# Second and third norm of a decoder step on one Trainium2 core: squares made block by block beside the products, two ones-products in place of eight, query product with the contraction outermost

## What is computed

```python
h += W_o [ attention heads | pooling groups ]( W_in rms_norm(h, norm_mix) )
h += mem_attend(rms_norm(h, norm_mem), mk, mv, w_mq, w_mo)     # second norm; q = xn @ w_mq, 4 heads of 128
tok = rms_norm(h, norm_ffn)                                    # third norm
h += moe(tok, router_w, router_b, w_up, b_up, w_down, b_down)  # top 4 of 32 experts, width 1024
y = rms_norm(h, norm_final)

def rms_norm(x, g):
    return x * rsqrt(mean(x * x, axis=-1) + EPS) * g
```

## Time and profile before

| | us |
|---|---|
| median of 3 runs | 1297.07 (1296.37 to 1297.4) |
| profiled execution, its own time | 1295.67 |
| its span in the trace | 1293.4 |
| PE busy | 1192.0 (92% of the span) |
| DVE busy | 389.3 (30%) |
| ACT busy | 223.8 (17%) |
| mean granted TensorE clock | 0.966 of full speed |

### The profile page before, as it was taken

How to read it: one execution, slowest core, us unless ns; L and a number is a source line. 1 busy time by engine, 2 the same in 40 slices (tenths; PEclk the granted TensorE clock), 3 DMA queues, 4 the chain that set the end, 5 groups by cost and what they waited for, 6 DMA issues and landing times.

```text
span 1293.4 us, 15539 instructions
## 1 busy us (share of the span) xinstructions
PE 1192.0 (92%) x6102; PEld 539.4 (42%) x6103; DVE 389.3 (30%) x921; ACT 223.8 (17%) x430; POOL 52.4 (4%) x67
## 2 busy tenths in 40 slices
PE   7997789798599999999899999999899999999997
PEld 5774555576433333333233333333333332333342
DVE  2376960241521222223122222312222231312222
ACT  1245640132111010111101011110101111110112
POOL 2117000000000000000000000000000000000000
PEclk9998698999689999999999999999999999999999
DMA  9234356306959999999999999999999999999993
GB/s 375 78 125 170 132 194 230 139 1 258 403 231 409 426 427 427 428 426 428 428 424 427 428 428 429 427 426 429 426 426 428 427 427 427 428 427 428 428 427 130
DMA packets 44220, 452.15 MB, mean 350 GB/s; under 512 B 5484, under 2 KB 6408, under 8 KB 18023
## 3 DMA queue, kind: packets, MB, share of 16 engines
q1 hardware_dynamic: 41711, 437.19, 80.8%
q0 software_dynamic: 2432, 13.89, 2.8%
HBM read 448.68 MB, written 2.61 MB: 349 GB/s over the span
## 4 chain that ended last, share of the span: by engine, by line
PE 70%; DVE 14%; DMA 10%; ACT 3%; issue 3%; POOL 0%; SPq 0%; DVEq 0%; ACTq 0%
PE psum L1194 26%; PE psum L1231 16%; DMA mem<-in_w_up_dram 10%; PE psum L1181 4%; PE psum L691 4%; DVE mem L2077 2%; PE psum L1148 2%; PE psum L989 2%; PE psum L896 2%; DVE mem L2069 2%; DVE mem L2072 1%; PE psum L1172 1%; DVE mem L1865 1%; ACT mem L1611 1%; DVE mem L2074 1%
## 5 line engine op out<-in xcount | busy, mean ns | idle before, releaser
L1194 PE MATMUL psum<-mem 128*64 128x512 f32 x2048 | 460.6, 601 | 12.8 <-DMA mem<-in_w_up_dram 6.3
L1194 PEld LDWEIGHTS psum<-mem 128*64 128x64 f32 x2048 | 144.7, 138 | 304.3 <-issue 291.0
L1231 PE MATMUL psum<-mem 128*64 128x512 f32 x1024 | 236.9, 600 | 0.0
L1231 PEld LDWEIGHTS psum<-mem 128*64 128x64 f32 x1024 | 66.6, 136 | 133.2 <-issue 112.6
L2069 DVE TENSOR_SCALAR mem<-psum 128x512 f32<-128x512 f32 x32 | 22.1, 692 | 272.6 <-PE psum L1194 272.6
L1611 ACT ACTIVATE mem<-mem 128x512 f32<-128x512 f32 x32 | 20.1, 629 | 470.7 <-DVE mem L2069 470.7
L1350 ACT ACTIVATE mem<-psum 128x512 f32<-128x512 f32 (+5 forms) x137 | 67.7, 545 | 153.6 <-PE psum L691 44.7
L2064 DVE TENSOR_TENSOR mem<-mem,psum 128x528 f32<-128x528 f32 x64 | 45.1, 704 | 143.7 <-PE psum L1181 143.7
L1181 PE MATMUL psum<-mem 128*128 128x264 f32 x256 | 65.5, 398 | 0.0
L1140 PE MATMUL psum<-mem 128*64 128x512 f32 x256 | 62.2, 607 | 2.4 <-DVE mem L2047 2.4
L2054 DVE TENSOR_SCALAR mem<-mem 128x64 f32<-128x64 f32 x102 | 25.6, 310 | 128.7 <-PE psum L1166 99.4
(11 more groups left out here) (310 smaller groups left out, 931.6 us busy)
## 6 DMA issues: line engine op xcount, KB each, us to landing
mem<-in_w_up_dram SPq DMA_DIRECT2D x128, 2048.0 KB, 30.5
mem<-in_w_down_dram SPq DMA_DIRECT2D x64, 2048.0 KB, 30.7
mem<-in_w_in_dram SPq DMA_DIRECT2D x8, 868.0 KB, 14.6
mem<-in_w_o_dram SPq DMA_DIRECT2D x1, 4096.0 KB, 14.4
mem<-in_cache_mem_k_dram SPq DMA_DIRECT2D x1, 4096.0 KB, 16.7
mem<-in_cache_mem_v_dram SPq DMA_DIRECT2D x1, 4096.0 KB, 14.2
mem<-in_w_mk_dram SPq DMA_DIRECT2D x1, 2048.0 KB, 8.7
mem<-in_w_mv_dram SPq DMA_DIRECT2D x1, 2048.0 KB, 14.8
```

Of the source, the lines that this page charges most:

```text
L1194: ins = pe.matmul(ps[64 * o:64 * o + 64, :], lhs, w[:, k % 2, g * 1024 + o * 512:g * 1024 + (o + 1) * 512], start=False, stop=(k == 7), sk ...
L1231: ins = pe.matmul(pso[64 * o:64 * o + 64, :], lhs, w[:, k % 4, o * 512:(o + 1) * 512], start=(k == 0), stop=(k == 7), skip_group_check=True)
```

## The change

ACT squares one feature block as soon as its sum is in `hT`, in eight instructions, and runs a small Sqrt ahead of them. DVE adds the squares of blocks 1 to 6 onto block 0, between its additions of the products. PE makes two ones-products, over the sum of blocks 0 to 6 and over block 7. Every scaling of the second and third norm now raises `xn_ready`; the query product has the feature block as its outer loop and waits block by block, the router product likewise in its first row tile.

```diff
--- before.py
+++ after.py
@@ -680,10 +680,10 @@
             def sum_squares(n):
 
                 b = take(pe, "ss", n)
-                pe.wait_ge(S("squares"), n - 1)
-                for k in range(KD):
-                    ins = pe.matmul(b[:, 0:NT], ones, xnT[:, k, :], start=(k == 0), stop=(k == KD - 1))
-                done(ins, "ss", n)
+                pe.wait_ge(S("squares_added"), (n - 1) * (KD - 2))
+                pe.matmul(b[:, 0:NT], ones, xnT[:, 0, :], start=True, stop=False)
+                pe.wait_ge(S("squares"), (n - 1) * KD)
+                done(pe.matmul(b[:, 0:NT], ones, xnT[:, KD - 1, :], start=False, stop=True), "ss", n)
 
             def z_rows(b, m, k):
 
@@ -1000,14 +1000,15 @@
                                            mknat[:, t, h * P:(h + 1) * P], ident)
                 done(ins, "mkT", g)
             sum_squares(2)
-            pe.wait_ge(S("xn_ready"), KD + 1)
             pe.wait_ge(S("w_mq_in"), 16)
-            for h in range(MH):
-                b = take(pe, "mq", h)
-                for k in range(KD):
-                    ins = pe.matmul(b[:, 0:NT], w_mq_sb[:, k, h * P:(h + 1) * P], xnT[:, k, :],
+            mqb = [take(pe, "mq", h) for h in range(MH)]
+            for k in range(KD):
+                pe.wait_ge(S("xn_ready"), KD + k + 1)
+                for h in range(MH):
+                    ins = pe.matmul(mqb[h][:, 0:NT], w_mq_sb[:, k, h * P:(h + 1) * P], xnT[:, k, :],
                                     start=(k == 0), stop=(k == KD - 1))
-                done(ins, "mq", h)
+                    if k == KD - 1:
+                        done(ins, "mq", h)
             for g in range(2):
                 wait_drained(pe, "mkT", g)
             for h in range(MH):
@@ -1090,10 +1091,11 @@
                 done(ins, "mo", m)
             sum_squares(3)
             b = take(pe, "rl")
-            pe.wait_ge(S("xn_ready"), KD + 2)
             pe.wait_ge(S("router_in"), 32)
             for r in range(3):
                 for k in range(KD):
+                    if r == 0:
+                        pe.wait_ge(S("xn_ready"), 2 * KD + k + 1)
                     ins = pe.matmul(b[0:ROWS[r], r * NE:(r + 1) * NE], xnT[:, k, r * P:r * P + ROWS[r]], rw_sb[:, k, :],
                                     start=(k == 0), stop=(k == KD - 1))
             done(ins, "rl")
@@ -1352,10 +1354,11 @@
                     ins.then_inc(drained(*job), 1)
                 return ins
 
-            def squares(n, waits):
-                for w in waits:
-                    wait_drained(act, *w)
-                act.activation(xnT, hT, ACT.Square).then_inc(S("squares"), 1)
+            def squares(n, tag):
+                act.activation(stat[:, 60:61], stat[:, 61:62], ACT.Sqrt)
+                for m in range(KD):
+                    wait_drained(act, tag, m)
+                    act.activation(xnT[:, m, :], hT[:, m, :], ACT.Square).then_inc(S("squares"), 1)
 
             def root(n):
                 b = result(act, "ss", n)
@@ -1529,7 +1532,7 @@
             for t in range(2):
                 b = result(act, "mv", t)
                 copy(mv[:, t, :], b[:, :], "mv", t)
-            squares(2, [("wo", m) for m in range(KD)])
+            squares(2, "wo")
             act.wait_ge(S("stored_mk"), 32)
             wait_filled(act, "mkT", 1)
             root(2)
@@ -1567,7 +1570,7 @@
             for s in range(2):
                 b = result(act, "smv", s)
                 copy(os_[:, s, :], b[:, :], "smv", s)
-            squares(3, [("mo", m) for m in range(KD)])
+            squares(3, "mo")
             root(3)
             for r in range(3):
                 w = ROWS[r]
@@ -1653,16 +1656,27 @@
                 for k in range(KD):
                     ins = dve.scalar_tensor_tensor(out=xnT[:, k, :], in0=hT[:, k, :], scalar=gains[:, gain + k:gain + k + 1],
                                                    in1=factor, op0=ALU.mult, op1=ALU.mult)
-                    if gain == 0:
-                        ins.then_inc(S("xn_ready"), 1)
-                return ins
+                    ins.then_inc(S("xn_ready"), 1)
 
             def norm(n, gain):
 
                 wait_drained(dve, "ss", n)
                 dve.reciprocal(temp[:, 2, :], temp[:, 3, :]).then_inc(S("rstd_ready"), 1)
                 dve.wait_ge(S("rstd_ready"), n - 1)
-                scale_tokens(gain, temp[:, 2, :]).then_inc(S("xn_ready"), 1)
+                scale_tokens(gain, temp[:, 2, :])
+
+            def add_product(n, tag, m):
+
+                b = result(dve, tag, m)
+                dve.tensor_tensor(hT[:, m, :], hT[:, m, :], b[:, 0:NT], ALU.add).then_inc(drained(tag, m), 1)
+                if 1 < m:
+                    add_squares(n, m - 1)
+
+            def add_squares(n, m):
+
+                dve.wait_ge(S("squares"), (n - 2) * KD + m + 1)
+                dve.tensor_tensor(xnT[:, 0, :], xnT[:, 0, :], xnT[:, m, :], ALU.add).then_inc(S("squares_added"), 1)
+                dve.wait_ge(S("squares_added"), (n - 2) * (KD - 2) + m)
 
             def ties(x, thr, k, gt, eq, cum, cnt, need, parts=P):
 
@@ -1913,8 +1927,7 @@
             dve.tensor_copy(mixT[0:64, 0:4, TP:NT], v[:, :, :, 0])
             dve.tensor_copy(mixT[64:128, 0:4, TP:NT], v[:, :, :, 1]).then_inc(drained("spo"), 1)
             for m in range(KD):
-                b = result(dve, "wo", m)
-                dve.tensor_tensor(hT[:, m, :], hT[:, m, :], b[:, 0:NT], ALU.add).then_inc(drained("wo", m), 1)
+                add_product(2, "wo", m)
             dve.wait_ge(S("stored_un"), 32)
             for m in range(KD):
                 wait_drained(dve, "wo", m)
@@ -1964,8 +1977,7 @@
                     ins = dve.tensor_copy(omT[:, h, TP + 4 * s:TP + 4 * s + 4], v[:, :, h])
                 ins.then_inc(drained("omt", s), 1)
             for m in range(KD):
-                b = result(dve, "mo", m)
-                dve.tensor_tensor(hT[:, m, :], hT[:, m, :], b[:, 0:NT], ALU.add).then_inc(drained("mo", m), 1)
+                add_product(3, "mo", m)
             for m in range(KD):
                 wait_drained(dve, "mo", m)
             norm(3, 16)
```

## The result

The changed kernel takes 1281.4 us (median of 4 runs, 1279.69 to 1282.87), the kernel before beside it 1296.72 us (4 runs, 1295.36 to 1297.4). The ratio is 0.9881, 95% interval 0.9868 to 0.9894: 1.2% faster, some 15 us. The forecast was 1281.1 us, from 1278.0 to 1285.5. The profiled execution is the slowest of the four, 1282.87 us with a span of 1281.0, so its trace accounts for 12.4 us of span, and not for 15; no trace shows the rest.

A forecast was written before the change was run, and what follows sets the result against it. Expert weight loading bounds the kernel, so the chain ahead of the first refill counts in full. Second norm 9.6 plus third norm 6.7 less bias wait 0.3 gives 16.0 us: 1297.07 to 1281.1 us, range 1278 to 1285.5.

The forecast's parts named there:

- The bound: Expert stage: weight loading holds it, so the end moves only with PE finishing its first part of weights.
- Second norm: Relay up to the query product: squares, ones-products, table load and scalings leave the chain, 8.5 us without the clock's term.
- The clock: PE around the second norm's gap: shorter idling may keep the clock up, gain 1.1 us, bounds 0 and 2.2.
- Third norm: Relay up to the router product: 7.25 us less, 6.7 us after 0.5 us given back in that product.
- the pace of the scalings: Router product's first row tile: runs only as fast as scalings arrive, giving back 0.5 us.
- Bias rows: Start of the expert stage: PE reaches `b_up` 6.7 us earlier with 6.4 us of slack, so waits 0.3 us.
- Rival (a): Start of the expert stage: late `b_up` or `b_down` swallows the third norm's gain, 1287.5 us; 7%.
- From the bias rows to the refill: First expert products: clock counted only as chance, about 1.8 us either way.
- (b): Both norms: additions of squares on DVE hold the ones-products, 2 us in each norm, 1285 us; 3%.
- (c): Expert loop: something other than the stream's start sets its end and takes all gain back, 1297 us; 1%.
- the constant: From PE's first finished part of weights to the end: time stays the same, no size given.
- The fourth: Second norm to attention: clock falls and stays down, query product 28.5 us in place of 16.4, whole 1320 us; 3%.

The follow-up runs named there:

- second_only: Changed kernel with the third norm kept as before, so only the second norm is changed; 1285.84 us, ratio 0.9924 to the kernel before.
- third_only: Changed kernel with the second norm kept as before, so only the third norm is changed; 1290.87 us, ratio 0.9953 to the kernel before.
- heads_outer: Changed kernel with the query product's head outermost again and one wait for all eight scalings; 1287.98 us, ratio 0.9930 to the kernel before.
- late_table: Changed kernel without the small Sqrt ahead of the squares, so the table loads behind the last square; 1282.14 us, ratio 0.9894 to before.
- bias_first: Changed kernel with `b_up` issued ahead of the first eight weight parts, no filler; 1280.83 us, ratio 0.9886 to the kernel before.
- eight_ones: Changed kernel with eight ones-products, each waiting for its own square, and no additions of squares; 1282.75 us, ratio 0.9899 to before.
- warm_both: Changed kernel with six useless ones-products as filler ahead of both query and router product; 1280.85 us, ratio 0.9886 to the kernel before.

## Why the prediction was right

**The bound.** Right, and the best supported step: the table above.

**Second norm.** The forecast was 8.5 us to the start of the query product; measured 8.36 (13.88 to 5.52 us). The square of a block took 0.42 us (0.39 taken). The additions of squares took 0.42 to 0.43 and held PE for 0.15. The table load was worth 1.29 and the seven scalings 2.78. The ones-products went from 3.80 to 1.13 us, 2.67 less where 2.85 was forecast. But that size holds only against the kernel before: with the squares made block by block, eight products would have cost only 2.28 us more in the second norm and 1.41 in the third, so a part of the term, half of it in the third norm, belongs to the squares.

**The clock.** I took 1.1 us of gain, the middle of 0 and 2.2; the 2.2 is the product's 16.40 us less 4 x 3.56 = 14.24 us. In the trace before, the clock fell to 0.50 at 253.5, 4.3 us after PE's last work and 2.9 ahead of the product. No run shows a gain of 1.1: in the trace after it was a loss of 0.8 us, outside my bounds. I had priced a fallen clock as "no worse than before", but here it fell at 247.0, just ahead of the query product, and covered 5.6 us of it; before, it covered 3.9. In the four other traces of an unfilled 3.21 us gap with this query order the clock fell to 0.50 too (in the gap in three of them, at 246.1, 246.5 and 247.7; in `second_only` at 246.7, 0.7 us into the product), and the product took 16.0 to 17.3 us against 16.4 before, so the term lies between a gain of 0.4 and a loss of 0.9. That a fallen clock costs about what was said is shown by the filler: 14.51 us, where I had 14.24. This is the mis-sized term of the sum.

**Third norm.** Forecast 7.25 us to the router product; measured 7.12 (12.40 to 5.28). Then I gave 0.5 us back for the pace of the scalings; the router product took 7.92 us in place of 7.96, so nothing was given back. I had divided 7.96 by 24, but the eight matmuls of the last tile, with 8 rows, are the short ones; the 16 others come every 0.43 us at this clock, about the 0.41 of the scalings.

**Bias rows.** Forecast a wait of 0.3 us, measured 1.01. The chain came 7.1 us earlier against the loads, but the slack was not 6.4 us. The second of the two `b_up` transfers is issued 0.46 us behind the first (318.15 in the trace before), and the 34.4 us run from there: it landed at about 352.5, and 5.9 us were left, with 0.1 for the hand-over. Rival (a), that this eats the whole of the third norm's gain, fell: PE waits for the excess over the slack alone, as `third_only` shows (1.32 us of 7.1), and the filler, whose 2 us shorter router product made the wait 2.2 us longer (3.24).

**From the bias rows to the refill.** The forecast put no mean on the clock in the first expert products, only 1.8 us of chance either way. From the start of the `b_up` products to the refill it was 9.2 us before, 10.0 and 11.5 in the two profiles of the changed kernel, 11.1 in `third_only`, 11.3 in `heads_outer`, 11.0 in `late_table`, 10.6 in `bias_first`; only `eight_ones`, with 8.5, was shorter. So with the third norm changed and no filler, six traces of seven lost 0.8 to 2.2 us here. The mean clock in the first up product was 0.68 before and 0.55 to 0.63 in the five that lost most.

**The other rivals.** (b) fell: in the second norm PE waits 0.15 us for the additions. In the third it stands idle for 1.03 us with the last addition as releaser, but that addition ends (310.78) no later than the last square (310.88), which the second product needs; both products stand behind them, as the forecast counted. (c) fell with the constant. The fourth, a clock that does not come back through the attention (3%), did not happen: in the trace after it was back at 1.00 at 253.8, within the query product.

**The sum.** In the profiled pair: 7.4 us by the first loads (forecast 9.6), 7.2 more up to the gather (6.7), 1.1 lost to `b_up` with its hand-over (0.3), and 0.8 lost between there and the refill, where the mean clock was 0.61 and had been 0.77, together 12.7 us at the refill and 12.4 in the span. The forecast's 16.0 is 3.3 us above that. The medians give 15.3. So the mechanism and the relay terms are right, within 0.2 us each, but that the forecast time lies within 0.3 us of the median is luck: in the trace after, the clock's term was 1.9 us too high, the bias rows and what follows them cost 1.6 us more than forecast, and the router's error of 0.5 us went the other way. The 2.5 us by which the medians gained more than the profiled pair (15.3 against 12.8) are in no trace.

## What to carry to other kernels

Ask what releases the long transfer-bound stage, and count every relay ahead of that moment in full; here 13 profiles agree within 0.41 us on what follows it. In a strict relay of engines, make the operand block by block under the producer and let the consumer start on the first block. Here that was worth more (1.5 and 2.8 us in a norm) than merging the products, and the parts share their gain: once the squares came block by block, merging gave 2.3 and 1.4 us. Before shortening the chain behind a transfer, look at the slack of small loads that are issued behind big ones, counted from the last of them: here `b_up` took 32.1 to 34.4 us to landing behind the first weights and 2.3 to 3.7 us ahead of them (`bias_first`). Once the slack was used up, what the chain gained turned into waiting (with the filler 2.0 us of router product gained, 2.2 us of wait added); issuing the small load first removed that wait, and with the filler a wait of 1.30 us for the next small load took its place.

## What the runs showed of the hardware

The clock fell within 2.0 us of PE's last work in the second norm of the trace after, with only two ones-products between idle times of 0.15 and 3.21 us, and 3.2 us after it in the third. The forecast had 2.5 us as the shortest, counted from 193; PE's last work there ended at 192.71 and the clock fell at 195.4, so it was 2.7.

The router product, 32 columns wide, took 7.92 us at 0.50 (after) and 5.94 us at a mean of 0.92 (`warm_both`), so its time depends on the clock. The 5.94 us are not its length at 1.00: in `warm_both` the first tile took 3.03 us, beside eight scalings of 3.32, and the second, with no scaling left to wait for, about 1.7 at the same clock. Where the product ran at 0.50, in the traces before and after, the clock did not come back during it, though PE was busy throughout; it came back during the transposes `xr` behind it. In the trace before that was at 342.2, just past the 12.3 us of the earlier trace rows and ahead of their end at 342.66. In the trace after it was at 325.4, where they run from 323.02 to 327.03:

```profile
324.00:325.00 1.00, 1.00 (x7) 1.00 (x6) 0.92 (x6) 0.60 (x1) 0.52 (x1) 0.50 1.06 442
325.00:326.00 1.00, 1.00 (x9) 0.98 (x9) 0.92 (x7) 0.96 (x2) 0.00 (x0) 0.77 0.77 328
326.00:327.00 1.00, 1.00 (x10) 0.60 (x7) 0.87 (x6) 0.99 (x2) 0.00 (x0) 1.00 1.20 508
```

Six ones-products of no use, 2.8 us of work in a gap of 3.2 us, held the query product at 14.51 us and the clock at 1.00 in all four traces with a filled second norm, and cost the chain nothing (5.43 to 5.44 us from `mkT`, 5.52 without). The same filler ahead of the router product gave 5.84 to 5.98 us in three traces and 7.83 in the fourth.
